# A feed-forward down-projection with tokens on the partitions instead of model columns, its sums turned back by transposes

## What is computed

```python
u = _rmsnorm(x, g_mlp) @ w_ff1              # 256 x 4096
x = x + jnp.square(jax.nn.relu(u)) @ w_ff2  # the down-projection, 256 x 4096 by 4096 x 1024
# second block
u = rmsnorm(x, norm_mix_pre_w)
q, k, v, ... = jnp.split(u @ w_in, ...)     # q, k and v of width 768 each
```

## Time and profile before

| | us |
|---|---|
| median of 3 runs (1190.92 to 1190.92) | 1190.92 |
| the profiled execution's own time | 1192.29 |
| its span | 1190.5 |
| PE busy in the span | 1179.1 (99%) |
| DVE busy | 829.2 (70%) |
| ACT busy | 664.2 (56%) |
| mean granted clock of TensorE | 0.998 |

### The profile page before, as it was taken

One profiled execution on the slowest core, in us unless ns is written; L12 is line 12 of the kernel. 1 busy time (PEld: TensorE's weight loads), 2 busy tenths in 40 slices (PEclk: granted clock), 3 DMA queues, 4 the chain that ended last, 5 costly groups with the idle time before them and its releaser, 6 DMA issues.

```text
span 1190.5 us, 19559 instructions
## 1 busy us (share of the span) xinstructions
PE 1179.1 (99%) x8398; PEld 1105.6 (93%) x8398; DVE 829.2 (70%) x952; ACT 664.2 (56%) x766; POOL 16.4 (1%) x34
## 2 busy tenths in 40 slices
PE   9999999999999999999999999999999999999998
PEld 8999999999888899999999999999988888999886
DVE  7867676787756567776547758999987557677543
ACT  7543545677553445544434558889885435555342
POOL 0000000000000000000000000000000000000000
PEclk9999999999999999999999999999999999999999
DMA  9553445556665645556564746556456644555651
GB/s 328 166 172 108 148 146 166 152 159 182 212 218 192 207 148 165 189 178 213 177 186 153 233 123 202 179 172 197 162 191 234 205 149 160 167 173 186 219 204 43
DMA packets 181269, 213.23 MB, mean 179 GB/s; under 512 B 6700, under 2 KB 147372, under 8 KB 181184
## 3 DMA queue, kind: packets, MB, share of 16 engines
q1 hardware_dynamic: 177696, 200.30, 52.5%
q0 software_dynamic: 2912, 10.79, 3.0%
q10 hardware_dynamic: 576, 0.90, 0.2%
HBM read 210.87 MB, written 1.09 MB: 178 GB/s over the span
## 4 chain that ended last, share of the span: by engine, by line
PE 87%; DVE 9%; ACT 3%; issue 1%; DMA 0%; DVEq 0%; ACTq 0%
PE ps L242 50%; PE ps L2013 20%; PE ps L2342 7%; PE ps L1764 5%; DVE w_lo L210 3%; DVE arena L1270 3%; PE ps L1813 1%; PE ps L1767 1%; ACT w_hi L204 1%; DVE arena L1593 1%; PE ps L2302 1%; DMA pcol<-in_params 0%; DVE arena L1609 0%; PE ps L2309 0%; DVE arena L1625 0%
## 5 line engine op out<-in xcount | busy, mean ns | idle before, releaser
L210 DVE TENSOR_TENSOR w_lo<-raw,w_hi 128x2048 fp32r<-128x2048 f32 x187 | 428.0, 2290 | 195.6 <-ACT w_hi L204 195.3
L242 PE MATMUL ps<-x_hi,w_hi 128*128 128x256 f32 x1760 | 506.5, 288 | 0.0
L242 PE MATMUL ps<-x_hi,w_lo 128*128 128x256 f32 x1760 | 498.3, 283 | 0.0
L242 PE MATMUL ps<-x_lo,w_hi 128*128 128x256 f32 x1760 | 498.2, 283 | 0.0
L204 ACT CAST w_hi<-raw 128x2048 fp32r<-128x2048 f32 x187 | 354.8, 1901 | 195.1 <-PE ps L2013 101.9
L242 PEld LDWEIGHTS ps<-x_hi,w_hi 128*128 128x128 f32 x1760 | 337.6, 192 | 4.0 <-issue 3.0
L242 PEld LDWEIGHTS ps<-x_lo,w_hi 128*128 128x128 f32 x1760 | 337.7, 192 | 0.7
L242 PEld LDWEIGHTS ps<-x_hi,w_lo 128*128 128x128 f32 x1760 | 337.5, 192 | 0.0
L2013 PE MATMUL ps<-w_hi,x_hi 128*128 128x512 f32 x344 | 135.1, 393 | 0.0
L2013 PE MATMUL ps<-w_lo,x_hi 128*128 128x512 f32 x344 | 134.0, 390 | 0.0
L2013 PE MATMUL ps<-w_hi,x_lo 128*128 128x512 f32 x344 | 134.0, 390 | 0.0
(11 more groups left out here) (244 smaller groups left out, 1193.7 us busy)
## 6 DMA issues: line engine op xcount, KB each, us to landing
raw<-in_w_in SPq DMA_DIRECT2D x170, 512.0 KB, 4.7
raw<-in_w_ff SPq DMA_DIRECT2D x64, 512.0 KB, 4.5
raw<-in_w_up SPq DMA_DIRECT2D x32, 512.0 KB, 4.3
raw<-in_w_down SPq DMA_DIRECT2D x32, 512.0 KB, 4.6
raw<-in_w_mem_kv SPq DMA_DIRECT2D x16, 512.0 KB, 6.1
raw<-in_w_out SPq DMA_DIRECT2D x16, 512.0 KB, 4.3
raw<-in_w_ssm_proj SPq DMA_DIRECT2D x16, 512.0 KB, 4.6
raw<-in_w_x_proj SPq DMA_DIRECT2D x8, 512.0 KB, 4.8
```

What stands on the lines that cost most here:

```text
L210: nc.vector.tensor_tensor(w_lo[:, s], raw[:, s], w_hi[:, s].bitcast(FP32), ALU.subtract)\
L242: last = nc.tensor.matmul(dst, l, r, start=start and k == 0 and m == 0, stop=stop and k == nk - 1 and m == 2)
```

## The change

The down-projection of the first block is done as `down2` is: 16 units of 24 matmuls with 512 streamed columns, eight units for the left half of the model width (banks 3 and 4, a bank for each 128 tokens), then eight for the right half (banks 5 and 6). ACT copies a finished half to `mixt` in SBUF (L831, two copies of 128 x 512), and TensorE turns it back by transposes of 128 x 128, four for each 128 tokens, into banks 0, 1, 3 and 4 as four quarters; DVE adds those to `res` where it added the banks before. The left half is turned after unit 9, the right half between parts of q and k: the first four row tiles of q's first half, four transposes, the same of k, four transposes, the same of q's second half. Since bank 1 then has two open sums, q's second half goes to bank 0, and its evacuation is two instructions. Bank 0 is v's, so v waits until q has been evacuated.

```diff
 # SP
-            deep("down", a["w_ff2"][0])
+            for b in range(16):
+                wide_load(U("down", b), a["w_ff2"][0], b % 8 * 4, b // 8 * 512)
 # ACT
+            def down_copy(c, t):
+                A(mixt[:, t, y_cols(c)], y_bank(c, t), ACT.Copy).then_inc(S("d_copy"), 1)
+            def down_high(p):
+                act.wait_ge(S(f"deep{p % 2}"), 2 + p // 2)
+                high(res, "norm_mix_pre_w_2", p, H0, "b_hi")
             hidden("up", 0)
-            deep(res, 0, 16, "norm_mix_pre_w_2")
+            for b in range(16):
+                split()
+                if b == 8:
+                    finished(act, U("down", 7))
+                    down_copy(0, 0)
+                    down_copy(0, 1)
+                if b == 11:
+                    for p in (0, 1):
+                        down_high(p)
+                        squares(res, 2 * p)
+            act.wait_ge(S("d_half"), 1)
+            down_copy(1, 0)
+            finished(act, U("down", 15))
+            down_copy(1, 1)
+            down_high(2)
+            down_high(3)
+            squares(res, 4)
+            squares(res, 6)
             split()
             inverse(1)
 # DVE
+            def down_added(p):
+                dve.wait_ge(S("d_t"), max(p, 1))
+                d = rows(res, 2 * p, 2)
+                tt(d, d, down_turned(p), ALU.add).then_inc(S(f"deep{p % 2}"), 1)
             hidden("up", 0)
-            deep("down", res, True, 1, 16, "norm_mix_pre_w_2")
+            for b in range(16):
+                split()
+                if b == 11:
+                    for p in (0, 1):
+                        down_added(p)
+                        down_low(p)
+                        pair(1, p)
+            down_added(2)
+            down_added(3)
+            down_low(2)
+            down_low(3)
+            pair(1, 2)
+            pair(1, 3)
             split()
...
-                tt(dst, unit_bank(u), bc(rs_row(), 2), ALU.mult).then_inc(taken(u), 1)
+                if n == 0:
+                    tt(dst[:, 0], unit_bank(u)[:, 0], rs_row(), ALU.mult)
+                    tt(dst[:, 1], bank(0, T), rs_row(), ALU.mult).then_inc(taken(u), 1)
+                else:
+                    tt(dst, unit_bank(u), bc(rs_row(), 2), ALU.mult).then_inc(taken(u), 1)
 # TensorE
-            deep("down", 0)
+            for b in range(16):
+                down(b)
+                if b == 9:
+                    down_turn(0, (0, 1))
...
             q, k, v = (U("att", 0, n, 3) for n in range(3))
-            half(q, 0, H0, lo=("b_lo", 0, 1))
+            late = ("b_lo", 0, 1)
+            begin(q)
+            pe.wait_ge(S("deep1"), 2)
+            products(pe, q, 0, H0, FP, 4, stop=False, lo=late)
+            down_turn(1, (0,))
+            begin(k)
+            products(pe, k, 0, H0, FP, 4, stop=False)
+            down_turn(1, (1,))
+            products(pe, q, 1, H0, FP, 4, out_=bank(0, T), stop=False)
+            products(pe, q, 0, H0, FP, lo=late, k0=4)
             norm_folded(1)
             norm(1, 3)
-            half(q, 1, H0)
-            unit(k, H0)
+            products(pe, q, 1, H0, FP, out_=bank(0, T), k0=4).then_inc(S(f"unit{q % SLOTS}"), 1)
+            products(pe, k, 0, H0, FP, k0=4)
+            products(pe, k, 1, H0, FP).then_inc(S(f"unit{k % SLOTS}"), 1)
+            evacuated(pe, q)
             half(v, 0, H2, TOK, lo=("n_lo", KT, 1))
```

More of the change, by code:

```diff
@@ L318, in y_bank, with down_turned @@
             return bank(3 + c * 2 + t, 512)
+        def down_turned(p):
+            return bank(p if p < 2 else p + 1, 2, T)
         def wide(w):
@@ L373, in plain @@
                     load(sp, U(stage, i), halves(w, 0, i * CW))
-            def deep(stage, w):
-                for i in range(16):
-                    load(sp, U(stage, i), halves(w, i % 4 * KT, i // 4 * CW))
             quarters(memt, a["mem_t"], "mem_in")
@@ L827, in hidden @@
                     A(rows(x_hi, 2 * c + U0, 2), cells(1024 + 512 * (c % 2), 2, T), ACT.Copy).then_inc(S("f_hi"), 1)
[L829 to L838, removed]
-            hidden("up", 0)
-            deep(res, 0, 16, "norm_mix_pre_w_2")
+            def down_copy(c, t):
[3 more added lines that the diff above has]
+                high(res, "norm_mix_pre_w_2", p, H0, "b_hi")
+            hidden("up", 0)
+            for b in range(16):
[16 more added lines that the diff above has]
+            squares(res, 6)
             split()
@@ L1482, in hidden, with down_low @@
                     low(2 * c + U0, q, "f_hi", c + c0 + 1, "f_lo")
[L1484 to L1497, removed]
+            def down_added(p):
+                dve.wait_ge(S("d_t"), max(p, 1))
+                d = rows(res, 2 * p, 2)
+                tt(d, d, down_turned(p), ALU.add).then_inc(S(f"deep{p % 2}"), 1)
+            def down_low(p):
+                lower(res, "norm_mix_pre_w_2", p, 0, H0, ("b_hi", "b_lo"))
             dve.wait_ge(S("n_r"), 1)
             hidden("up", 0)
-            deep("down", res, True, 1, 16, "norm_mix_pre_w_2")
+            for b in range(16):
[11 more added lines that the diff above has]
+            pair(1, 3)
             split()
@@ L2073, in norm, with down_turn, down @@
                     last.then_inc(S("n_ss"), 1)
[L2075 to L2086, removed]
+            def down_turn(h, tokens):
+                for t in tokens:
+                    pe.wait_ge(S("d_copy"), 2 * h + t + 1)
+                    for k in range(4):
+                        last = tr(down_turned(2 * h + k // 2)[:, k % 2, t * P:(t + 1) * P],
+                                  mixt[:, t, (4 * h + k) * P:(4 * h + k + 1) * P])
+                        if t == 1 and k in ((3,), (1, 3))[h]:
+                            last.then_inc(S("d_t"), 1)
+            def down(b):
+                u, c = U("down", b), b // 8
+                begin(u)
+                pe.wait_ge(S("f_lo"), 2 * (b % 8 + 1))
+                for t in range(2):
+                    for k in range(4):
+                        for m, (wt, xt) in enumerate(((w_hi, x_hi), (w_hi, x_lo), (w_lo, x_hi))):
+                            last = nc.tensor.matmul(y_bank(c, t), xt[:, U0 + 4 * (b % 8) + k, t * P:(t + 1) * P],
+                                                    wide(wt[:, u % SLOTS])[:, k],
+                                                    start=b % 8 == 0 and k == 0 and m == 0,
+                                                    stop=b % 8 == 7 and k == 3 and m == 2)
+                    if b == 15 and t == 0:
+                        last.then_inc(S("d_half"), 1)
+                last.then_inc(S(f"unit{u % SLOTS}"), 1)
             u, v = U("out", 0), U("out", 1)
```

## The result

| | before | after |
|---|---|---|
| median, runs side by side (6 each) | 1191.62 us | 1196.36 us (1195.99 to 1197.35) |
| profiled execution's own time | 1192.29 | 1196.24 |
| its span | 1190.5 | 1194.4 |
| PE busy | 1179.1 | 1178.4 |

The ratio is 1.004, with a 95% interval of 1.0029 to 1.005: slower by 0.3 to 0.5%. The prediction had 1192.9 us, a range up to 1196.0, and 0.55 for slower.

A forecast was written before the change was run, and what follows sets the result against it. The prediction took TensorE's own stream, busy 99%, as the bound. It summed -5.20 + 1.76 + 0.55 + 0.54 + 4.36 = +2.0 us, giving 1192.9 us against the median of 1190.92, with a range of 1190.5 to 1196.0.

The forecast's parts named there:

- The wide form and the transposes: Down-projection: 512-column matmuls save 5.20 us over 16 units; one group of eight transposes and two of four cost 1.76 us.
- The formula that gives 0.96 for the saving: The skill's N/2.4 + 2.5 ns from start to start, saving only 2.5 ns a pair; the prediction took the trace instead.
- Work costed at nothing: In the stage, ACT's copies, DVE's handling of both left quarters and SP's loads make TensorE wait for nothing.
- none at unit 14: Unit 14's weights are ready 2.4 us before TensorE needs them, so no hole there.
- The seam's chain: Between the blocks: some twenty operations from the last addition to q's evacuation, timed step by step, making TensorE pause three times.
- The three pauses: TensorE's waits at the seam: 0.55 us for `x_lo` tiles, 0.54 for the norm's sums, 4.36 before v.
- nothing waits behind v's start: After v starts, TensorE is later against DVE than before, so no further wait follows.
- the chance of the clock: Rival: the clock falls in the pause before v, costing 1.4 us, up to 2.8; total 1194.3, up to 1195.7; chance 0.22.
- the case without a fall: The main forecast: +2.0 us from stage and seam with no clock loss, 1192.9 us; chance 0.55.
- the third pause: At the seam in front of v, TensorE waits 4.36 us for q's evacuation, with TensorE still for about 4.2 us.
- The prediction's 1.4 to 2.8: Price in us of a clock fall behind the third pause, taken from slow weight loads at the program's start.
- The case with a fall: The clock rival: half clock behind the pause before v, total +3.4 us, 1194.3 us, up to 1195.7; chance 0.22.

The follow-up runs named there:

- run with matmuls in the hole: The changed kernel with 30 never-read matmuls of 256 columns in front of v's wait for q's evacuation; 1194.67 us, ratio 1.0023 to the kernel before.
- bank 5 form with the earlier cast: The changed kernel with q's second half in bank 5 and ACT's cast of v's weights moved ahead of DVE's addition; 1190.36 us, ratio 0.9986 to before.
- the form with q's second half done whole: The changed kernel with q's second half done whole behind the norm's sums, needing no second bank; 1191.66 us, ratio 0.9993 to before.
- before with the added wait: The kernel before, with v's first matmul also waiting for q's evacuation; 1193.88 us beside 1192.24, ratio 1.0016.

## Why the prediction was wrong

Point by point, by its own steps:

- **The wide form and the transposes**: -5.20 + 0.88 for the stage, -4.32; measured 87.96 - 92.14 = -4.18. Right. The formula that gives 0.96 for the saving has no support in it.
- **Work costed at nothing**: no hole in the stage, none at unit 14. Right.
- **The seam's chain.** Counted from the start of unit 15, which is 631.04 - 5.44 = 625.60 in the profile after, the prediction had the addition at 9.17, the scaling at 16.72, q's evacuation at 23.33 and v at 24.13. In DVE's and TensorE's rows these are 9.17, 16.68, 23.29 and 24.09:

```profile
634.77 1.28 DVE L1503 TENSOR_TENSOR res<-res,ps 128x512 f32<-128x512 f32 x2 [4.68 <-PE ps L1793]
...
642.28 1.29 DVE L1474 TENSOR_TENSOR arena<-res,arena 128x512 f32<-128x512 f32 x2
...
648.89 0.42 DVE L1585 TENSOR_TENSOR arena<-ps,arena 128x256 f32<-128x256 f32 x1
```

  The three pauses, from where the next row would have started, were 0.58, 0.46 and 4.28 us, for 0.55, 0.54 and 4.36. Durations of rows, in each engine's written order, carried over twenty operations within 0.1 us. The claim that nothing waits behind v's start held too. So the part of "slower" that rests on the seam was right by its mechanism: without the fall in the seam the change still costs 2.2 us where 2.0 was forecast, as the run with matmuls in the hole shows.
- **The step that failed: the chance of the clock.** The forecast was the case without a fall, at 0.55, which puts the cost of the lowered clock at nothing; the fall was given 0.22, with the reasons that its one case was at the end of the span and that none stood in mid-kernel. One did, after a pause of 2.90 us that is shorter than the 4.2 forecast here. With that row the fall behind the third pause would have been the likelier case, and its price could have been read off too: 1.37 us between the profiled execution and the median. The prediction's 1.4 to 2.8, taken from the start of the program, held: with the fall shown by the windows and taken away by the matmuls in the hole, 1.5 is measured. The stretch of TensorE's timeline ahead of `up2` was not read, because the page says 99% busy and the prediction looked for holes only at the seam.
- **The base of the sum.** The prediction noted that the profiled execution was 1.37 above the median and did not ask why. The three runs were at the level without a fall at the start of `up2`. The profile of after has that fall too (granted clock 0.50 between 1006 and 1008). By the profiles the change costs 3.9 us: -4.2 for the stage, +7.9 at the seam, the rest (0.3) before the stage's start. By the medians it is 4.7, and 4.0 to 5.4 by the level at which before stood. The case with a fall, named at 1194.3, was thus 1.4 too low in its base: from 1192.29 it comes to 1195.7, and the other 0.5 us to the profiled 1196.24 is mostly the 0.3 ahead of the stage and 0.1 each in the stage and in the clock's price. The median, 1196.36, lies 0.4 above the range's upper end of 1196.0.

## What to carry to other kernels

A bank borrowed to cover one wait can put a longer one in the place where its owner comes next: before an open sum is moved to another bank, look up in the timeline when the engine that empties it will be there. When an execution differs from the median by a fixed step, find that step in the trace before building on either; here it was a clock that fell behind a pause, the same mechanism that took the change beyond its forecast. On an engine that is 99% busy the one or two holes that remain are the rows to read first.

## What the runs showed of the hardware

- The granted clock can go to half after TensorE has begun again: in the changed kernel v's matmuls started at 649.69 at full rate, and the fall came at about 650.3. A still engine's price can therefore stand behind the hole, in matmuls that wait for nothing. It need not: in the bank 5 form with the earlier cast the clock fell at about 998.5, ahead of the first matmul of `up2` at 999.01.
- A pause of 2.90 us ahead of `up2` stands in eight of the profiled executions. In six the clock fell (before among them), in two it did not (the form with q's second half done whole, and before with the added wait: granted clock 1.00 there). At the seam 4.12 us was followed by a fall, 2.94, 1.23 and 0.52 by none. The clock was at half for about 3.4 us each time, which cost 1.4 to 1.5. The Trainium skill ("TensorE: Matmul & The Clock Gate", section "Why this matters for your kernels") advises against idle gaps between bursts of matmuls; the runs agree, and show besides that products whose result nobody reads, put into the gap, buy the time back (1.5 us at the seam, and the upper level ahead of `up2`).
- The 512-column form costs 226.8 ns from start to start in the chain (54.43 us for 240) where the 256-column form costs 120.0, in stages with the same casts beside them: a fixed part of 13 ns a matmul. The Trainium skill ("TensorE: Matmul & The Clock Gate", section "Back-to-back issue gap") puts it at 2.5 ns in its formula, which it gives for matmuls apart from a stream; these streams do not agree with it.
